# Latent attention loop of a two-layer mixer kernel: the merge products moved to the second and fourth unit of each head

## What is computed

```python
kv = (ckv_all @ p['mla_w_ukv'][l]).reshape(b, -1, MLA_HEADS, MLA_NOPE + MLA_V)
y_mla = mla_attention(q_nope, q_rope, kv[..., :MLA_NOPE], kr_all, kv[..., MLA_NOPE:])
...
br = jnp.stack([y_hy, y_da, y_mla], axis=2) * jax.nn.silu(paths.reshape(b, n, N_BRANCH, BR_W))
y_br = jnp.einsum('blni,nid->blnd', br, p['w_branch'][l])
merged = jnp.sum(jax.nn.sigmoid(merge.reshape(b, n, N_BRANCH, D_MODEL)) * y_br, axis=2)
```

## Time and profile before

| | |
|---|---|
| time, median of 3 runs | 1883.45 us (1882.04 to 1885.08) |
| span of the profiled execution | 1881.3 us |
| median less span (what lies around the span) | 2.15 us |
| TensorE busy | 1776.7 us, 94% of the span |
| TensorE weight load busy | 1588.9 us, 84% |
| VectorE busy | 1156.0 us, 61% |
| ScalarE busy | 681.7 us, 36% |
| GpSimd busy | 476.8 us, 25% |
| mean granted TensorE clock | 0.987 of full speed |
| the chain that ended last | 67% TensorE, 19% VectorE, 5% ScalarE |

### The profile page before, as it was taken

One profiled execution on the slowest core, in us unless ns is written; L12 is line 12 of the kernel. 1 busy time (PEld: TensorE's weight loads), 2 busy tenths in 40 slices (PEclk: granted clock), 3 DMA queues, 4 the chain that ended last, 5 costly groups with the idle time before them and its releaser, 6 DMA issues.

```text
span 1881.3 us, 28233 instructions
## 1 busy us (share of the span) xinstructions
PE 1776.7 (94%) x11464; PEld 1588.9 (84%) x11464; DVE 1156.0 (61%) x1620; ACT 681.7 (36%) x1174; POOL 476.8 (25%) x230
## 2 busy tenths in 40 slices
PE   5899999999899999999989999999998999999996
PEld 3887899878798888999877969998887888889996
DVE  5599894545354544576977989925544654435745
ACT  3424312434234544322363242224432554442122
POOL 0100032212242211467200000421122412125551
PEclk9999999999999999999989999999999999999998
DMA  9111121211211111354520112211112111115431
GB/s 355 45 56 34 34 101 62 62 40 52 69 36 56 38 41 53 135 191 143 219 94 30 57 34 79 79 57 51 40 34 93 33 48 53 43 45 186 137 109 63
DMA packets 50448, 150.04 MB, mean 80 GB/s; under 512 B 9674, under 2 KB 13898, under 8 KB 49552
## 3 DMA queue, kind: packets, MB, share of 16 engines
q1 hardware_dynamic: 46720, 134.09, 21.0%
q10 hardware_dynamic: 3600, 14.16, 2.1%
HBM read 141.63 MB, written 6.59 MB: 79 GB/s over the span
## 4 chain that ended last, share of the span: by engine, by line
PE 67%; DVE 19%; issue 5%; ACT 5%; DMA 2%; POOL 2%; SPq 0%; ACTq 0%; DVEq 0%; POOLq 0%
PE PS L836 16%; PE PS L837 15%; PE PS L841 15%; PE PS L908 4%; PE PS L897 3%; PE PS L1093 2%; PE PS L939 2%; PE PS L942 2%; PE PS L921 2%; DVE Wl L1578 1%; ACT Wh L1216 1%; POOL Wl L2019 1%; DVE work L1551 1%; DVE work L1550 1%; DVE MG L1823 1%
## 5 line engine op out<-in xcount | busy, mean ns | idle before, releaser
L2019 POOL TENSOR_TENSOR Wl<-W,Wh 128x1024 fp32r<-128x1024 f32 (+3 forms) x178 | 372.4, 2093 | 1236.5 <-ACT Wh L1216 1197.2
L836 PE MATMUL PS<-Hh,Wh 128*128 128x320 f32 x2048 | 615.7, 315 | 26.4 <-ACT Wh L1216 21.2
L837 PE MATMUL PS<-Hl,Wh 128*128 128x320 f32 x2048 | 607.3, 311 | 0.0
L836 PEld LDWEIGHTS PS<-Hh,Wh 128*128 128x128 f32 x2048 | 388.7, 190 | 50.1 <-ACT Wh L1216 25.2
L837 PEld LDWEIGHTS PS<-Hl,Wh 128*128 128x128 f32 x2048 | 388.8, 190 | 0.2
L841 PE MATMUL PS<-Hh,Wl 128*128 128x320 f32 x2048 | 321.3, 309 | 0.6 <-POOL Wl L2019 0.6
L841 PEld LDWEIGHTS PS<-Hh,Wl 128*128 128x128 f32 x2048 | 305.6, 188 | 0.9 <-POOL Wl L2019 0.8
L1557 DVE TENSOR_REDUCE st<-PS 128x1 f32<-128x640 f32 (+1 forms) x160 | 114.9, 718 | 277.0 <-PE PS L921 155.9
L1216 ACT ACTIVATE work<-PS 128x640 f32<-128x640 f32 (+8 forms) x276 | 169.6, 624 | 214.0 <-PE PS L841 67.5
L1216 ACT ACTIVATE Wh<-W 128x1024 fp32r<-128x1024 f32 (+3 forms) x210 | 188.3, 900 | 89.1 <-DMA W<-in_w_in 34.8
L1373 ACT ACTIVATE th<-PS 128x640 f32<-128x640 f32 x64 | 45.0, 703 | 341.6 <-PE PS L841 341.6
(11 more groups left out here) (253 smaller groups left out, 2587.3 us busy)
## 6 DMA issues: line engine op xcount, KB each, us to landing
W<-in_w_in SPq DMA_DIRECT2D x132, 512.0 KB, 3.5
W<-in_w_branch SPq DMA_DIRECT2D x48, 256.0 KB, 2.6
work<-in_w_mod_rows ACTq DMA_DIRECT2D x23, 512.0 KB, 3.9
pmod_w<-in_w_mod SPq DMA_DIRECT2D x8, 1024.0 KB, 11.3
W<-in_w_out SPq DMA_DIRECT2D x16, 512.0 KB, 4.2
work<-in_x_sample SPq DMA_DIRECT2D x2, 2048.0 KB
late_modulation_w<-in_w_mod_rows SPq DMA_DIRECT2D x5, 512.0 KB, 6.7
x_mid<-work SPq DMA_DIRECT2D x1, 2560.0 KB, 8.5
```

The costliest lines, as they stand in the source:

```text
L836: pe.matmul(out, Wh[:, b, kk, :], xh[:, kk, t], start=kk == 0, stop=False)
L837: pe.matmul(out, Wh[:, b, kk, :], xl[:, kk, t], start=False, stop=False)
L2019: return pool.tensor_tensor(out, in_, high.bitcast(f32), ALU.subtract)
```

## The change

A new argument `marks` says how many fillers stand behind unit t of each head. With `(0, 1, 1, 2, 2)` the gate product comes behind the score of unit 1 and the branch product behind the score of unit 3. The last `ml_weights` moves from the step of the last branch product to the step `ml_ptrans` 38, behind the last score. `SLOT` and `UPTO` follow from the new list. Nothing that is computed changes.

```diff
-def attention_steps(tag, heads, fillers, before=None, behind=None, full=False, cover=((), ())):
+def attention_steps(tag, heads, fillers, before=None, behind=None, full=False, cover=((), ()), marks=None):
...
-        upto = min(t, 3) + 1 + 4 * h if full else len(fillers) * (u + 1) // len(units)
+        upto = min(t, 3) + 1 + 4 * h if full else marks[t] + marks[-1] * h if marks else len(fillers) * (u + 1) // len(units)
         steps += fillers[taken:upto]
...
-    s += [step for t in range(NT) for step in head(0, t)] + attention_steps("ml", MH, merge_steps(1), head)
+    s += [step for t in range(NT) for step in head(0, t)] + attention_steps("ml", MH, merge_steps(1), head, marks=(0, 1, 1, 2, 2))
...
                         g = 12 * n_ + 4 + d
-                        if i == 2 * KD - 1:
-                            ml_weights(l, MH * NT - 1)
                         dve.wait_ge(*filled(l, kind, i))
...
                         if i == 3 * NT + 1:
                             turn_queries(l, 1)
+                    elif (kind, i) == ("ml_ptrans", MH * NT - 2):
+                        ml_weights(l, MH * NT - 1)
                     elif kind in ("xt", "xta", "xtb"):
```

## The result

The changed kernel takes 1900.47 us in the median of four runs (1898.87 to 1902.25) against 1882.74 for the kernel before: ratio 1.0092, 95% interval 1.0078 to 1.0107. It is slower, by 12 to 18 us; 8.2 were forecast.

The account below looks back on a forecast made before the run. TensorE was taken to bound the kernel, at 94% of the span. New waits of 13.88 us less 9.79 removed gave +4.1 us a layer, +8.2 in all, 1891.6 us; own range 1888.5 to 1896, widened to 1884 to 1896.

Parts of the forecast that it names:

- wait 1: End of heads 0, 4, 6: unit 3's transposition waits for VectorE's weights, its add held by GpSimd; 1.38 us, three times, 4.14.
- old waits: All TensorE waits in one loop of the kernel before, 9.79 us a layer, all counted as removed by the change.
- 0.14 of the first gate product: Head 0: the first gate product was read as waiting 0.14 us, counted among the removed waits.
- New wait 2: End of heads 1, 3, 5: unit 3's transposition waits for ScalarE's second key copy to free its PSUM slot; 1.49 us, three times, 4.47.
- New wait 3: Heads 2, 4, 6, 7: the values product waits for ScalarE's copy of the context weights; 0.45 us, four times, 1.80.
- GpSimd 1.12 behind its start, -0.54: In wait 1: GpSimd starts the next gate tile's low part 0.54 us before the branch product ends, 1.12 behind ScalarE's high-part start.
- with GpSimd 0.5 later: Bound on waits 1 and 4: GpSimd 0.5 later costs 4 us more, sum +12.2 us.
- New wait 4: End of the loop: last transpositions and values product wait, no branch product between them and the last score; 3.47 us.
- Work in it is 1.88, wait 3.47: Loop's end: values product starts 5.35 us behind the last branch product, with 1.88 us of work and 3.47 of wait between.
- (c): Rival: inner changes cancel and only the loop's end costs, 2.39 us a layer, +4.8, 1888.2 us; chance 18%.
- (a): Rival: faster, if the six waits at heads' ends (waits 1 and 2) average under 0.75 us; -9.0, 1874.4 us; chance 10%.

Follow-up runs that it names:

- gate-only kernels: Kernel before with only the gate product moved, to behind the score of unit 1: 1871.8 us, ratio 0.9936; with further ScalarE reorderings 1869.2 and 1863.8 us.
- last two corrections: Gate product moved alone, plus ScalarE's context copy before the branch tile's high part (1869.2 us), plus that high part one place earlier in heads 1, 3, 5 (1863.8 us).
- filled end: Changed kernel with 20 matmuls, results overwritten, added in TensorE's two waits at each loop's end: 1892.5 us, ratio 1.0049 to the kernel before.
- low part behind add: Changed kernel, but GpSimd begins the low part of the tile behind a branch product only after VectorE's add: 1917.1 us, ratio 1.0176 to the kernel before.
- low part behind scaling: Changed kernel, but GpSimd begins the low part of gate and path tiles only after VectorE's scaling of unit 3: 1890.3 us, ratio 1.0024 to the kernel before.

## Why the prediction was wrong

The sign and the four new waits were right, the size was too small: +8.2 us forecast, 13.1 us in the loops, 12.4 to 17.7 us measured, outside the range. Two steps failed: the lower clock at the end of the loop was in no term, and wait 1 was priced alike for head 0.

- *The old waits, 9.79 us a layer, all removed.* Right but for the 0.14 of the first gate product. That was no wait: it takes 7.28 us in the changed kernel too, since in these traces a product directly behind a score is 0.14 longer and the score 0.24 shorter. In the gate-only kernels the others go as read, and with the last two corrections the loop is 178.93, 8.25 us under the old one.
- *New wait 2, behind the keys product.* Right: transposition at 5.91, forecast 5.97; taking the high part out of ScalarE's queue took out 0.9 us each.
- *New wait 3, the values products.* Right to 0.01 us (1.64); putting the copy first removed it.
- *New wait 1, behind the even heads.* The mechanism was right, and heads 4 and 6 came at 3.80 for 3.69. In head 0 it came at 4.79. The failed step: "GpSimd 1.12 behind its start, -0.54", taken for all three heads. In head 0 VectorE, ScalarE and GpSimd are later (GpSimd at +0.59), the add took 2.52 us and the wait was 2.48 instead of 1.38, and the bound "with GpSimd 0.5 later" was too narrow for a start that was 1.1 later.
- *New wait 4, the end.* Failed step: "Work in it is 1.88, wait 3.47", with the values product behind it at its usual length. The wait was 3.64, and the clock fell to half behind it: 1.68 us a layer more, 3.4 in all, absent from the sum and from the range. The filled end shows the cause: with matmuls in the two idle stretches the clock stayed at 1.00.
- *The sum.* Per layer: 4.1 forecast, + 1.7 for the clock, + 1.1 for head 0, + 0.2 for heads 4 and 6, + 0.2 for the end, - 0.2 for the keys, + 0.1 for the 0.14 that stayed gives 7.2. Measured were 6.5. The missing 0.7 is that a score followed directly by a product hands over faster: 0.84 + 7.29 = 8.13 for a score and a gate product, where apart they take 1.08 + 7.15 = 8.23. The change brings that about in seven heads, 0.1 each (in head 0 it was so before). The other steps come out even.
- *The rivals.* (c), only the end costs, was the wrong cut: the end costs 4.1 us a layer, the inside 2.4 (189.6 less 187.2). (a) asked for six waits under 0.75 on average; they were 1.6. A gain came only where the gate product moved alone. The two moves were not priced apart, though each new wait had its owner: waits 1, 2 and 4 appear with the branch product alone, wait 3 with the gate product alone.

## What to carry to other kernels

Price each moved piece by itself: here one half of the move was worth -11 us of loop time and the other +16. Then price them together, since they need not add: both came to +13, not +5. Before spacing out filler work, ask what each filler covered; the branch product at the end of a head covered ScalarE's two key copies, VectorE's add and scaling, and the clock. And where GpSimd works beside VectorE, look which of VectorE's instructions its next one will meet; it can be made to wait until the critical one is through, but not merely until the one before it is.

## What the runs showed of the hardware

- TensorE's clock fell to half in the middle of a kernel, at the end of each loop, in the changed kernel behind idle stretches of 2.31 and 0.85 us with transpositions between them. The same was seen behind 3.28 and 0.75 us (low part behind add) and behind 1.74 and 0.37 (low part behind scaling). In these runs the product behind took 3.77 to 4.88 us instead of 2.52.
- Behind a single idle stretch of 2.20 us it fell in two of the heads of the run with the low part behind the add (the gate product behind took 8.79 and 8.40 us instead of 7.29), and behind 2.21 in head 0 of the same run, and 2.24 in head 0 of the changed kernel, it did not. So the length of one idle stretch does not decide it by itself.
- A VectorE scaling of 128 columns, 0.29 us, took 2.27 us when it began 0.16 us behind the start of a GpSimd subtraction of 2.35 us, and one of 640 columns, 0.55 us, took 2.21 when it began 0.48 behind the start of one of 2.34.
- 20 matmuls put into TensorE's waits made each loop 1.65 us shorter (193.74 to 192.09).
